# Rotary halves of fifteen blocks exchanged by SBUF transfers instead of matrix products, heads started three places behind a rotation, and that stage's weight loads issued by ScalarE

## The reference, cut to what matters

```python
def apply_rope(x, cos, sin):
    half = x.shape[-1] // 2
    x1, x2 = x[..., :half], x[..., half:]
    ...
    return jnp.concatenate([x1 * c - x2 * s, x2 * c + x1 * s], axis=-1)

def diff_attention(hn, w_qkv, w_o, lq1, lk1, lq2, lk2, subln_g, lambda_init, cos, sin):
    qkv = hn @ w_qkv
    q, k, v = jnp.split(qkv, [DIFF_QK_WIDTH, 2 * DIFF_QK_WIDTH], axis=-1)
    q = apply_rope(q.reshape(B, S, 2 * H, d), cos, sin).reshape(B, S, H, 2, d)
    k = apply_rope(k.reshape(B, S, 2 * H, d), cos, sin).reshape(B, S, H, 2, d)
    ...
        p = jax.nn.softmax(s, axis=-1)
        a = p[:, :, 0] - lam * p[:, :, 1]
        return jnp.einsum('bhqk,bkhe->bqhe', a.astype(v.dtype), v)
    ...
    o = rms_norm(o, subln_g, SUBLN_EPS) * (1.0 - lambda_init)
    return o.reshape(B, S, DIFF_V_WIDTH) @ w_o
```

## Time and profile before

| | |
|---|---|
| three runs | 1133.47, 1134.96 and 1135.14 us, median 1134.96 |
| the profiled execution | 1133.52 us, span 1132.2 us |
| TensorE busy | 1119.0 us, 99% of the span |
| VectorE, ScalarE, GpSimd busy | 822.3 us (73%), 637.5 us (56%), 56.8 us (5%) |
| granted TensorE clock | 0.999 of full speed (2.4 GHz) |
| chain that ended last | TensorE 86%, VectorE 5%, ScalarE 5%, transfers 2% |

### The profile page before, as it was taken

One profiled execution on the slowest core, in us unless ns is written; L12 is line 12 of the kernel. 1 busy time (PEld: TensorE's weight loads), 2 busy tenths in 40 slices (PEclk: granted clock), 3 DMA queues, 4 the chain that ended last, 5 costly groups with the idle time before them and its releaser, 6 DMA issues.

```text
span 1132.2 us, 16844 instructions
## 1 busy us (share of the span) xinstructions
PE 1119.0 (99%) x6542; PEld 980.1 (87%) x6542; DVE 822.3 (73%) x1416; ACT 637.5 (56%) x1203; POOL 56.8 (5%) x68
## 2 busy tenths in 40 slices
PE   8999999999999999999999999999999999999997
PEld 6998989799988888888899988888889988888886
DVE  6988878798666766676777867666667866766665
ACT  6664444856757755555755556544556654555553
POOL 2200000000001000000012300000001100000000
PEclk9999999999999999999999999999999999999999
DMA  9989999594232766668453326555554434655530
GB/s 385 419 317 380 321 368 263 226 344 154 104 113 75 243 212 221 221 223 208 145 187 112 117 108 224 186 189 186 190 182 166 167 112 149 213 189 192 191 128 37
DMA packets 36992, 231.10 MB, mean 204 GB/s; under 512 B 6825, under 2 KB 8241, under 8 KB 9522
## 3 DMA queue, kind: packets, MB, share of 16 engines
q1 hardware_dynamic: 31536, 225.59, 56.7%
q10 hardware_dynamic: 5378, 4.45, 1.3%
HBM read 228.95 MB, written 1.07 MB: 203 GB/s over the span
## 4 chain that ended last, share of the span: by engine, by line
PE 86%; DVE 5%; ACT 5%; DMA 2%; issue 1%; POOL 1%; ACTq 0%; DVEq 0%; POOLq 0%
PE ps L1722 43%; PE pacc L1722 42%; DVE wlo L2274 1%; ACT whi L2002 1%; DMA raw<-in_stream 1%; ACT arena L2109 1%; ACT wk L2212 1%; DMA cl<-in_cols 1%; POOL st L2604 1%; DVE st L2499 0%; PE ps L1861 0%; DVE wk L2493 0%; DVE wlo L2284 0%; PE ps L1932 0%; DVE h L2390 0%
## 5 line engine op out<-in xcount | busy, mean ns | idle before, releaser
L2274 DVE TENSOR_TENSOR wlo<-raw,whi 128x1024 fp32r<-128x1024 f32 x346 | 414.9, 1223 | 115.3 <-ACT whi L2002 115.1
L1722 PE MATMUL ps<-both,whi 128*128 128x256 f32 (+2 forms) x1728 | 460.7, 339 | 1.4 <-DVE both L2365 0.6
L2002 ACT ACTIVATE whi<-raw 128x1024 fp32r<-128x1024 f32 x346 | 360.4, 1056 | 100.6 <-PE ps L1722 46.5
L1722 PE MATMUL ps<-both,wlo 128*128 128x256 f32 x1264 | 354.6, 281 | 0.0
L1722 PEld LDWEIGHTS ps<-both,whi 128*128 128x128 f32 (+1 forms) x1728 | 296.9, 189 | 41.9 <-issue 3.1
L1722 PEld LDWEIGHTS ps<-both,wlo 128*128 128x128 f32 x1264 | 238.8, 189 | 2.9
L1722 PE MATMUL pacc<-whi,both 128*128 128x512 f32 (+2 forms) x352 | 106.4, 383 | 1.0 <-ACT both L2125 0.6
L2002 ACT ACTIVATE sg<-ps 128x256 f32<-128x256 f32 (+1 forms) x98 | 37.3, 380 | 100.2 <-PE ps L1722 100.2
L2294 DVE SCALAR_TENSOR_TENSOR raw<-raw,silu_c 128x1024 f32<-128x1024 f32 x72 | 89.9, 1256 | 1.8 <-DMA raw<-in_stream 1.6
L1722 PE MATMUL pacc<-whi,mhi 128*128 128x512 f32 x228 | 90.7, 398 | 0.0
L1722 PE MATMUL pacc<-whi,mlo 128*128 128x512 f32 x228 | 89.5, 392 | 0.0
(11 more groups left out here) (280 smaller groups left out, 1471.9 us busy)
## 6 DMA issues: line engine op xcount, KB each, us to landing
raw<-in_stream SPq DMA_DIRECT2D x213, 1024.0 KB, 5.0
gates<-gate_rows ACTq DMA_DIRECT2D x3, 512.0 KB, 6.6
h<-in_x SPq DMA_DIRECT2D x2, 512.0 KB, 4.2
cst<-in_const ACTq DMA_DIRECT2D x1, 1024.0 KB, 4.7
arena<-bias_rows ACTq DMA_DIRECT2D x1, 1024.0 KB, 25.9
arena<-in_final_g SPq DMA_DIRECT2D x1, 512.0 KB, 5.8
out<-tmp SPq DMA_DIRECT2D x2, 256.0 KB, 2.0
out<-tmp ACTq DMA_DIRECT2D x2, 256.0 KB, 2.3
```

Of the source, the lines that this page charges most:

```text
L1722: return e.matmul(o, a, b, start=start, stop=stop)
L2002: return e.activation(o, a, ACT.Copy, **how)
L2274: return e.tensor_tensor(o, a, hi.bitcast(F32), ALU.subtract)
```

## The change

For fifteen of the sixteen blocks (all but the k block of the last head) the halves are exchanged by transfers. ScalarE copies the block to one of three slots in `arena` (step `rope_swap`), SyncE waits for that copy and issues four transfers of 32 partitions each (1 KB per partition) inside SBUF, and GpSimd's cosine product reads the copy. The closing (`rope_close`: VectorE's sine product, now from SBUF, and the adds) is written one block later in the list. The signs move from the permutation into the sine table. The heads' distance `rest[0]` is 3 instead of 2 in this stage, and its weight loads are issued by ScalarE, each behind the next block's copy, so that SyncE's program holds only the exchanges there.

```diff
+    def load_chunk():
+        if loader[0] == "act":
+            owed.append(0)
+        else:
+            load_next()
+
+    def load_owed():
+        while owed:
+            owed.pop()
+            load_next()
...
+    def swapped(dst, split, b, tk, s, by):
+        slot = slots.take()
+        n, (at, t_tables) = slot.at, by
+        x, y = tick("rpc"), tick("rpz")
+        swaps[n] += 64
+        add("rope_swap", b=b.at, full=tk, s=s, n=n, free=slot.free, at=at, tables=t_tables, copied=x)
+        banks.give(b, x)
+        yield
+        sine = tick("rps")
+        add("rope_close", n=n, cosine=y, swapped=(f"swap{n}", swaps[n]), sine=sine, at=at, dst=dst, split=split)
+        t = tick("rpd", 2 if split else 1)
+        slots.give(slot, t)
+        yield t
...
+    pending, rest[0], loader[0] = [], 3, "act"
     for hh in range(8):
         for g in (0, 8):
...
-            rope = roped(("kT", hh) if g else ("qT", hh), not g, b, tk, 1.0 if g else 0.125, by_r)
+            last = g and hh == 7
+            rope = (roped if last else swapped)(("kT", hh) if g else ("qT", hh), not g, b, tk, 1.0 if g else 0.125, by_r)
             next(rope)
+            load_owed()
             side.nudge()
             feed()
-            side.soon(rope_end(g + hh, rope))
+            if pending:
+                at, was = pending.pop()
+                t_q[at], born[at] = next(was), side.now
+            if last:
+                side.soon(rope_end(g + hh, rope))
+            else:
+                pending.append((g + hh, rope))
+    load_owed()
+    loader[0] = "sp"
+    rest[0] = 2
...
+        elif st.kind == "rope_swap":
+            q.wait_ge(*st.copied)
+            x, s, _ = m.swap_slot(st.n)
+            for a in range(0, P, 32):
+                c = a ^ 32
+                e.dma_start(s[a:a + 32, :], x[c:c + 32, :]).then_inc(S[f"swap{st.n}"], 16)
...
+        elif kind == "rope_swap":
+            q.wait_ge(*st.full)
+            q.room(st.free)
+            copy(m.swap_slot(st.n)[0], m.bank(st.b)[:, 0:T], scale=st.s).then_inc(S["rpc"], 1)
...
+        elif kind == "rope_close":
+            what, h = st.dst
+            _, s, y = m.swap_slot(st.n)
+            q.wait_ge(*st.swapped)
+            q.wait_ge(*st.cosine)
+            o = s if st.split else m.kT[:, h, :]
+            e.tensor_tensor(o, s, m.rope_table(st.at, "sin"), ALU.mult).then_inc(S["rps"], 1)
+            q.wait_ge(*st.sine)
...
+        elif kind == "rope_swap":
+            q.wait_ge(*st.copied)
+            q.wait_ge(*st.tables)
+            x, _, y = m.swap_slot(st.n)
+            e.tensor_tensor(y, x, m.rope_table(st.at, "cos"), ALU.mult).then_inc(S["rpz"], 1)
```

More of the change, by code:

```diff
@@ L243, in gains_of, with load_next @@
         return []
+    owed, loader = [], ["sp"]
     def load_chunk():
+        if loader[0] == "act":
[6 more added lines that the diff above has]
+            load_next()
+    def load_next():
         n = pos["chunk"]
@@ L250, in load_chunk @@
         free = [t for u in (2 * (n - NR), 2 * (n - NR) + 1) for t in raw_free.get(u, [])]
-        add("load", chunk=n, free=latest(*free))
+        add("load", chunk=n, free=latest(*free), lane=loader[0])
     def feed(until=None, limit=100):
@@ L1276, in roped @@
         yield t
+    slots, swaps = Places([Place(n) for n in range(3)]), Counter()
+    def swapped(dst, split, b, tk, s, by):
[11 more added lines that the diff above has]
+        yield t
     turns, by_r = [], []
@@ L1544 @@
     "xsq", "xg", "xnew", "xrow", "xz", "xzd", "xah", "xhi", "xlo", "phi", "plo", "fin", "wa", "wb",
-    "ixc", "ixt", "mod", "g8", "masks", "tabc",
+    "rpc", "rpz", "swap0", "swap1", "swap2", "ixc", "ixt", "mod", "g8", "masks", "tabc",
     "lows", "sums", "sg", "hm", "hhi", "hlo", "rsilu", "rgate",
@@ L1626, in __init__, with swap_slot @@
         self.fg = self.arena[:, 6144:7168]
+    def swap_slot(self, n):
+        x, y = self.view(4096, 8, T), self.view(11776, 3, T)
+        return x[:, n, :], x[:, 3 + n, :], y[:, n, :]
     def view(self, at, n, width):
@@ L1698, in sync_program @@
     for st in steps:
-        if st.kind == "load":
+        if st.kind == "load" and st.lane == "sp":
             q.room(st.free)
@@ L2018, in scalar_program @@
                 copy(hi, raw).then_inc(S["hi"], 1)
+        elif kind == "load" and st.lane == "act":
+            q.room(st.free)
+            n = st.chunk % NR
+            e.dma_start(m.raw[:, n, :], d["stream"][st.chunk]).then_inc(S[f"raw{n}"], 16)
         elif kind == "opening":
@@ L2537, in vector_program @@
                 e.tensor_tensor(o, o, y, ALU.add).then_inc(S["rpd"], 1)
+        elif kind == "rope_close":
[6 more added lines that the diff above has]
+            q.wait_ge(*st.sine)
+            if st.split:
+                for c, r in enumerate(LOHI):
+                    e.tensor_tensor(m.qT[r, 2 * h + c, :], s[r, :], y[r, :], ALU.add).then_inc(S["rpd"], 1)
+            else:
+                e.tensor_tensor(o, o, y, ALU.add).then_inc(S["rpd"], 1)
         elif kind == "lambda":
@@ L2654, in constants @@
     for m in range(P):
[L2655 to L2658, removed]
+        r[m + 32 if m % 64 < 32 else m - 32, m] = 1.0
     put("rot", r)
@@ L2667, in constants @@
     put("cos", np.cos(ang).astype(np.float32).T[i % 32])
-    put("sin", np.sin(ang).astype(np.float32).T[i % 32])
+    put("sin", np.sin(ang).astype(np.float32).T[i % 32] * np.where(i % 64 < 32, -1.0, 1.0)[:, None].astype(np.float32))
     t = np.arange(T)
```

## The result

The changed kernel takes 1138.06 us (median of 5 runs, 1137.41 to 1140.50) against 1133.57 for the kernel before in the same session (1133.43 to 1135.14). The ratio is 1.0038, with a 95% interval of 1.0023 to 1.0053: slower by about 0.4%, near the forecast of 1138.6 us.

A forecast was written before the change was run, and what follows sets the result against it. VectorE was taken to bind the stage: two collisions (0.44, 0.54) less 0.17 us on the adds make its cycle 10.81 instead of 10.00 us. The end comes 3.65 us later, median 1138.6 us, own range 1136.6 to 1141.6.

The forecast's parts named there:

- VectorE sets the stage: In the stage, VectorE's 10.81 us per head binds; TensorE, needing 8.59, waits about 2.2 us per head for it.
- lead is used up over two heads: TensorE's lead of some 4 us over VectorE, losing 2.2 us per head, is gone after about two heads.
- First collision: GpSimd's first cosine product starts 0.32 us behind the reciprocal and holds VectorE's mix for 0.44 us per cycle.
- Second collision: GpSimd's second cosine product, 0.47 us behind its copy's start, holds VectorE's sine product for 0.54 us per cycle.
- my own list of signs: Expected in the profile: TensorE waits about 2.2 us per head, reciprocals 10.8 apart, mix over 1.1, sine product near 1.0.
- The adds: VectorE's adds lose their present small collisions, about 0.17 us per cycle (0.96 to 0.87, 0.51 to some 0.43).
- Exchanges at nothing: Transfers land in about 4 us, before their closings, and cost nothing; only the first may cost about 1 us.
- The rival of the late exchange: Each q block's closing waits for transfers beside 1 MB weight loads; six heads lose 1.1 us each, 1145 us; chance 0.10.
- my own signs of being wrong: Wrong if reciprocals come under 10 us apart, the mix keeps 0.75 us, or VectorE waits for transfers.
- The extra subtraction ahead of head 0: One more VectorE weight subtraction, 1.13 us, moves head 0's reciprocal from 592.41 to 593.54.
- The sum: From head 0's reciprocal to head 7's mix, VectorE's cycles add up to a kernel end 3.65 us later.

The follow-up runs named there:

- e7: Kernel before the change, with the scaling of six heads' values moved from VectorE to ScalarE; 1134.11 us, ratio 1.0000 to the kernel before.
- e4: Changed kernel without the sixty transfers; closings multiply the copied, unexchanged block by the sine table; 1134.97 us, ratio 1.0017 to the kernel before.
- e2: Changed kernel with GpSimd's cosine product of an exchanged block waiting for VectorE's last mix; 1140.90 us, ratio 1.0065 to the kernel before.
- e5: Changed kernel with GpSimd's cosine product taken just before its block's closing, after the closing before it; 1137.60 us, ratio 1.0032 to the kernel before.
- e9: Changed kernel with the first 1 MB weight load that ScalarE issues put one block later; 1140.16 us, ratio 1.0052 to the kernel before.
- e1: Changed kernel with head 0's two blocks rotated by product as before, the other thirteen by transfers; 1136.77 us, ratio 1.0022 to the kernel before.
- e3: Changed kernel with the edits of e1 and e2 together; 1137.89 us, ratio 1.0035 to the kernel before.
- e10: Changed kernel with e1 and e6, blocks closed two copies later, both cosine products beside the maxima; 1143.86 us, ratio 1.0087 to the kernel before.
- e12: e10 with a fourth place for blocks in exchange, the cosine product written over the copy; 1135.95 us, ratio 1.0018 to the kernel before.
- e6: Changed kernel with the scaling of six heads' values moved from VectorE to ScalarE; 1135.83 us, ratio 1.0019 to the kernel before.

## Why the prediction was right, point by point

- **VectorE sets the stage: right.** TensorE stands still for 7.76 us in it, mostly at the add of k (6.4 us), as named, and its transposition of head 7 starts 0.05 us behind that head's mix (667.43 and 667.38), as the sum assumes. (The profile counts no wait of TensorE behind 654.08 us, so that this rests on these two times and on the constant distance of the two lengths.) But per head it stands for 0.9 to 1.1 us at the add (not at all at head 2), not for about 2.2, and its busy time is 4.33 us less where the rotations were put at 6.45; I haven't traced the rest of these. Two sharper readings came out. In the kernel before TensorE was level with VectorE: VectorE waited 1.1 us for it, and lightening VectorE there gains nothing (e7). So neither engine alone could give more than about 1 us. And no lead is used up over two heads: TensorE stands at head 0 already, behind the late exchange, and without the transfers (e4) from head 1 on (0.99 us).
- **First collision: right,** at 0.32 us behind the reciprocal, and 0.40 us per head against 0.44.
- **Second collision: wrong, and this step failed.** I let GpSimd start the second cosine product 0.47 us behind its copy, and the copy does come where I put it (1.91 us behind the reciprocal, 1.95 forecast). But GpSimd works through one list, and the previous head's root stands ahead of that product (632.25, then 632.90). Only at head 0, where there is no root yet, does it happen. The mechanism itself is right (e2: 0.53 us); the place was read from ScalarE's rows alone. By my own list of signs, a sine product near 1.0 us, this part didn't come.
- **The adds: right,** 0.42 and 0.87 us, 0.18 less per cycle against 0.17.
- **Exchanges at nothing: wrong for the first.** I gave it 0 to 1 us; it cost 3.07. The issue is 0.59 us and not 0.33, and the landing 5.45 beside a load and not 4. All the others cost nothing (e4). The rival of the late exchange was thus real at one block of fifteen, and one of my own signs of being wrong, VectorE waiting for transfers, came true there. The section of the Trainium skill on who interferes with whom (SBUF — State Buffer) is borne out by e2 and e5 as to which instructions hold each other, again with a hold shorter than the whole instruction: in e2 the sine product ended 0.28 us behind the cosine product (630.56 and 630.28), less than its own 0.42.
- **The extra subtraction ahead of head 0: right.** It, and 2.19 us more of waits, put head 0's reciprocal at 15.37 us behind the scaling; I had 13.09 (593.54 - 580.45).
- **The sum: right by two errors that cancel.** Forecast against measured: head 0 13.09 and 15.37 (+2.28); head 0 to 4 41.11 and 39.29 (-1.82); head 4 to 7 28.83 and 27.78 (-1.05); reciprocal of head 7 to its transposition 1.13 and 1.36 (+0.23). Together -0.36: 3.65 us were forecast and 3.29 found, which the stretch behind makes 3.43. That the size came out is therefore luck: which engine sets the stage was understood, but a loss in every head and a single wait at the first one stood in for each other.

What stays open: the medians lie 4.5 us apart, 1 us more than the stage explains. The step ahead of the stage varies by more than that from execution to execution, and I have not separated the two.

## What to carry to other kernels

Before work is taken off a busy engine, add up what the other engines wait for it: here VectorE waited 1.1 us for a TensorE that was busy all the time, and that was the whole prize. When an operand moves from PSUM to SBUF, look at what GpSimd runs beside it, and find the place of GpSimd's instruction from its own list, not from when its input is ready. Price small transfers from their count (here 0.63 us of the issuing engine for each), and look for a bulk load beside the first one that has no slack.

## What the hardware showed that I had not expected

- Issuing a 32 KB transfer from SBUF to SBUF took SyncE 0.59 us (median of 60), where a 1 MB load takes 0.33. Landing took 1.8 to 5.5 us there, the longest beside a load (e9).
- After TensorE had been busy for 3.05 of 6 us, its granted clock was 0.50 for the next 6 us (1.2 GHz instead of 2.4), though it had work again (e9). In e1, e3, e5, e10 and e12 it fell in one stretch each, behind a pause of TensorE (0.51 to 0.65 in the lowest 3 us, 0.98 over its length). In the changed kernel it didn't fall, though TensorE was busy for only 0.79 of the 3 us from 592 to 595, nor in e10 with 0.55 of the 3 us from 644 to 647.
- GpSimd's root of 128x2 took 1.60 us beside a weight subtraction that started 0.17 us ahead of it, against 0.69 elsewhere (e6).
